# Three reorderings in a one-core, two-block transformer kernel: a projection tile ahead of a turned softmax, half a gate tile ahead of a suffix sum, and attention outputs split ahead of the next pair's logs

## The reference, cut to what matters

```
att = einsum(q * exp(b - b_mid), k * exp(b_mid - b));  att = where(causal, att, 0)
kv  = einsum(k * exp(b_last - b), v);  states by state = decay * state + kv
o   = att @ v + (q * exp(b)) @ states          # then a norm over each head and a gate
y   = softmax(q k / 8 + bias) v                # 8 heads
```

```
z = q k * 64 ** -0.5
log_beta = log_sigmoid(z);  log_rem = where(mask, log_sigmoid(-z), 0)
after = cumsum(log_rem, reverse) - log_rem
a = where(mask, exp(log_beta + after), 0);  o = a @ v
merged = sigmoid(gates[:1024] + b) * (o_diff @ w_o_diff) + sigmoid(gates[1024:] + b) * (o_sb @ w_o_sb)
```

## Time and profile before

| | |
|---|---|
| median of three runs | 1620.82 us |
| the profiled execution | 1622.88 us, its span 1621.1 us |
| PE busy, share of the span | 1449.0 us, 89% |
| DVE busy | 763.2 us, 47% |
| ACT busy | 578.3 us, 36% |
| mean granted TensorE clock | 0.949 |
| chain that ended last | PE 66%, DMA 18%, DVE 10%, ACT 4% |
| mixer, from the end of vm to the merge | 131.6 to 223.7 us |
| stick-breaking loop and what leads to it, layer 0 | 873 to 951 us |
| the same, layer 1 | 1286 to 1364 us |

### The profile page before, as it was taken

One profiled execution on the slowest core, in us unless ns is written; L12 is line 12 of the kernel. 1 busy time (PEld: TensorE's weight loads), 2 busy tenths in 40 slices (PEclk: granted clock), 3 DMA queues, 4 the chain that ended last, 5 costly groups with the idle time before them and its releaser, 6 DMA issues.

```text
span 1621.1 us, 23932 instructions
## 1 busy us (share of the span) xinstructions
PE 1449.0 (89%) x10631; PEld 1206.0 (74%) x10631; DVE 763.2 (47%) x1088; ACT 578.3 (36%) x708; POOL 2.9 (0%) x8
## 2 busy tenths in 40 slices
PE   7998999899767777677899899999999988999998
PEld 5696899755433434333888799999988878999997
DVE  2546564421101101101786676666367757765642
ACT  2452552221100100000546655434243665544431
POOL 0000000000000000000000000000000000000000
PEclk9997999999988988889999999999999999999999
DMA  6553147499999999999534335556534323546540
GB/s 206 208 187 120 53 156 314 185 406 426 427 427 426 427 427 427 425 427 416 180 131 150 111 107 177 185 169 221 192 121 141 119 105 117 195 156 204 188 155 27
DMA packets 116272, 374.56 MB, mean 231 GB/s; under 512 B 7767, under 2 KB 53127, under 8 KB 103623
## 3 DMA queue, kind: packets, MB, share of 16 engines
q1 hardware_dynamic: 112199, 370.70, 59.6%
q0 software_dynamic: 528, 2.04, 0.4%
q10 hardware_dynamic: 3440, 0.25, 0.2%
HBM read 371.92 MB, written 1.06 MB: 230 GB/s over the span
## 4 chain that ended last, share of the span: by engine, by line
PE 66%; DMA 18%; DVE 10%; ACT 4%; issue 1%; ACTq 1%; SPq 1%; DVEq 0%
PE bank L605 33%; DMA ring<-in_w_exp_up 10%; PE bank L1161 7%; PE bank L629 4%; DVE parts L1640 3%; PE bank L979 3%; DMA tail_hn<-in_w_exp_up 3%; DMA SZ<-in_w_exp_up 3%; PE bank L827 2%; DMA ring<-in_w_in 2%; PE bank L949 2%; PE bank L1006 2%; PE bank L583 2%; PE bank L651 2%; ACT parts L1255 1%
## 5 line engine op out<-in xcount | busy, mean ns | idle before, releaser
L605 PE MATMUL bank<-hnr,parts 128*128 128x256 f32 x4032 | 500.0, 286 | 7.6 <-DVE Gr L1792 6.8
L605 PEld LDWEIGHTS bank<-hnr,parts 128*128 128x128 f32 x4032 | 492.9, 194 | 13.4 <-DVE Gr L1792 7.2
L1640 DVE TENSOR_TENSOR parts<-ring,parts 128x2048 fp32r<-128x2048 f32 x148 | 333.7, 2288 | 129.4 <-ACT parts L1255 127.9
L1255 ACT ACTIVATE parts<-ring 128x2048 fp32r<-128x2048 f32 x146 | 271.5, 1902 | 105.5 <-PE bank L1161 58.7
L979 PE MATMUL bank<-ring,TMP 128*32 128x512 f32 x608 | 88.9, 734 | 47.9 <-DMA ring<-in_w_exp_up 47.2
L605 PE MATMUL bank<-SKr,parts 128*128 128x256 f32 x960 | 119.9, 288 | 8.6 <-DVE SKr L2031 5.8
L605 PEld LDWEIGHTS bank<-SKr,parts 128*128 128x128 f32 x960 | 118.6, 196 | 9.2 <-issue 9.1
L1161 PE MATMUL bank<-Gr,parts 128*128 128x256 f32 x640 | 115.3, 283 | 0.0
L1986 DVE COPY KV<-bank 128x256 f32<-128x256 f32 x16 | 6.8, 425 | 219.7 <-PE bank L966 219.7
L979 PEld LDWEIGHTS bank<-ring,TMP 128*32 128x32 f32 x608 | 23.5, 130 | 105.4 <-issue 90.2
L1161 PEld LDWEIGHTS bank<-Gr,parts 128*128 128x128 f32 x640 | 99.9, 192 | 0.0
(11 more groups left out here) (324 smaller groups left out, 1637.4 us busy)
## 6 DMA issues: line engine op xcount, KB each, us to landing
ring<-in_w_in SPq DMA_DIRECT2D x60, 1024.0 KB, 7.3
ring<-in_w_ffn_in SPq DMA_DIRECT2D x44, 1024.0 KB, 7.3
ring<-in_w_exp_gate SPq DMA_DIRECT2D x19, 2048.0 KB, 39.7
ring<-in_w_exp_up SPq DMA_DIRECT2D x19, 2048.0 KB, 44.2
ring<-in_w_exp_down SPq DMA_DIRECT2D x18, 2048.0 KB, 39.3
ring<-in_w_ffn_out SPq DMA_DIRECT2D x20, 1024.0 KB, 6.1
G<-in_w_exp_gate SPq DMA_DIRECT2D x7, 2048.0 KB, 38.6
tail_hn<-in_w_exp_up SPq DMA_DIRECT2D x7, 2048.0 KB, 43.1
```

Of the source, the lines that this page charges most:

```text
L605: m = mm(b(name)[:, T * half:T * half + T], part(chunk, ws)[:, k, P * mt:P * mt + P], src[xs][:, k, :], start=k == 0 and i == 0, stop=k == ...
L1255: A(parts[:, 2 * (r % 2), 2048 * i:2048 * i + 2048], ring[:, CHUNK[chunk][0], 2048 * i:2048 * i + 2048], ACT.Copy).then_inc(high_made, 1)
L1640: v.tensor_tensor(parts[:, 2 * (r % 2) + 1, at], ring[:, CHUNK[chunk][0], at], parts[:, 2 * (r % 2), at].bitcast(F32), ALU.subtract).then_ ...
```

## The change

There are five moves; no instruction is added or taken away but for waits. (1) The 48 matmuls of zg0 go ahead of mt_0. (2) In the mixer, DVE does the products with the decays ahead of low(zg0), vm0 and vm1, and low(zg1) after both norms; PE's waits for v1 and vm1 go to where they are used; ACT does high(zg1) after the first two softmaxes, and waits for io ahead of reading zg0, since z1 overlays the states. (3) Ahead of the loop in each layer, the first of ga1's two tiles goes ahead of ba0. (4) In the loop, second_highs goes ahead of sb_exps on ACT and second_lows ahead of sb_logs_of on DVE. (5) The second half of high(gb1) goes ahead of the gate bias of head 3.

```diff
-    g += [..., "ke", "ko", "mt_0", "oe", "oo", "ie", "io", "ms2"]
-    g += ["zg0", "gn0", "gn1", "mo0", "mt_1", "ms3", "zg1"]
+    g += [..., "ke", "ko", "zg0", "mt_0", "oe", "oo", "ie", "io", "ms2"]
+    g += ["gn0", "gn1", "mo0", "mt_1", "ms3", "zg1"]
...
 PE, mixer
-            emptied(pe, "v1")
-            emptied(pe, "vm1")
             causal_scores("ms0", qm, km, 0)
...
             emptied(pe, "kt")
+            emptied(pe, "v1")
             (ke, ko)
+            group_f("zg0", "zg0", 0)
             pe.wait_ge(prob_ready, 1)
             causal_turn("mt_0", prob[0])
             (oe, oo, ie, io)
             causal_scores("ms2", qm, km, 2)
-            group_f("zg0", "zg0", 0)
...
+            emptied(pe, "vm1")
             moba_out(0)
...
 PE, layers
                 diff_turn(3)
+                split_tile("ga0" + x, hn_parts, "ga1" + x, 2)
                 sb_after_sum(0)
-                group_f("ga0" + x, "ga1" + x, 1)
+                split_tile("ga0" + x, hn_parts, "ga1" + x, 3)
...
 ACT, mixer
             high("zg0")
-            high("zg1")
             take("kt", kdt.rearrange("p a b -> p (a b)"))
             causal_exp(0, [prob[0]])
             causal_exp(1, [prob[1]])
+            high("zg1")
             take_turned("mt_0", 0)
+            full(act, "io")
             take("zg0", two(z1, 0))
...
 ACT, loop over h
+                    if h in (2, 4, 6):
+                        second_highs(f"bo{h // 2 - 1}{x}", h // 2 - 1)
                     if h in (0, 2, 4):
                         sb_exps(h + 2)
                     if h < 7:
                         sb_weights(h + 1)
                     if h in (0, 2, 4):
                         sb_softplus(h + 2)
-                    if h in (2, 4, 6):
-                        second_highs(f"bo{h // 2 - 1}{x}", h // 2 - 1)
...
+                    if h == 3:
+                        high("gb1" + x, [1])
                     (gates)
-                    if h in (2, 3):
-                        high("gb1" + x, [h - 2])
+                    if h == 2:
+                        high("gb1" + x, [0])
...
 DVE, mixer
             take("km1", two(km, 1))
-            low("zg0")
-            take("vm0", vm[:, 0, :])
-            take("vm1", vm[:, 1, :])
             (products with the decays, memsets)
+            low("zg0")
+            take("vm0", vm[:, 0, :])
+            take("vm1", vm[:, 1, :])
...
-            low("zg1")
             moba_logits(0)
             (ae, ao)
             moba_logits(1)
+            moba_norm(0)
             (states)
-            moba_norm(0)
             moba_norm(1)
+            low("zg1")
...
 DVE, loop over h
                         sb_mask(h + 1)
+                    if h in (2, 4, 6):
+                        second_lows(f"bo{h // 2 - 1}{x}", l + 1, h // 2 - 1)
                     if h in (0, 2, 4):
                         sb_logs_of(h + 2)
                         sb_logs_of(h + 3)
...
-                    if h in (2, 4, 6):
-                        second_lows(f"bo{h // 2 - 1}{x}", l + 1, h // 2 - 1)
```

More of the change, by code:

```diff
@@ L117, in group_plan @@
     g += ["qk0", "qk1", "alr", "v0", "v1", "alpha", "r0", "r1", "qm0", "qm1", "km0", "km1", "vm0", "vm1"]
-    g += ["kt", "ms0", "ae", "ao", "ms1", "ke", "ko", "mt_0", "oe", "oo", "ie", "io", "ms2"]
-    g += ["zg0", "gn0", "gn1", "mo0", "mt_1", "ms3", "zg1"]
+    g += ["kt", "ms0", "ae", "ao", "ms1", "ke", "ko", "zg0", "mt_0", "oe", "oo", "ie", "io", "ms2"]
+    g += ["gn0", "gn1", "mo0", "mt_1", "ms3", "zg1"]
     for h in range(2, 8):
```

## The result

| | before | after |
|---|---|---|
| median (lowest to highest, runs) | 1621.07 us (1620.76 to 1622.02, 4) | 1591.74 us (1590.83 to 1592.65, 4) |
| the profiled execution, its span | 1622.88 us, 1621.1 us | 1591.38 us, 1589.6 us |
| PE busy | 1449.0 us | 1434.4 us |
| DVE, ACT busy | 763.2, 578.3 us | 762.5, 578.0 us |
| mean granted clock | 0.949 | 0.959 |

The ratio of the times is 0.982, with a 95% interval of 0.9805 to 0.9835. The kernel became 29.3 us faster; forecast were 1593.3 us and a gain of 27.5. PE does the same matmuls in 14.6 us less. Not all of that is gain: 3.8 us of it lie between the mixer's merge and layer 0, a stretch that is only 0.8 us shorter. In the stretches that the change reorders, up to the merges, PE is idle for 18.7 us less and busy for 14.3 us less; in the merges of the two layers it is busy for 4.1 us more. DVE and ACT do the same work.

What follows compares the result with a forecast made beforehand. TensorE holds two thirds of the chain of waits, DMA most of the rest; PE's waits and slow clock were the target. Mixer 9.5 + layers 18 = 27.5 us off 1622.88 gives 1595.4, as a median 1593.3; range 1583 to 1606.

Steps and rivals of the forecast that it cites:

- The walk: Layer 0's loop, followed step by step in its trace: merge starts at 940.5 instead of 951.15, 10.7 us gained.
- The walk of DVE's tail: Layer loop: DVE's work from Ln's end at 919.0 through the first first_lows, 21.4 us, making PE wait 2.6 at the merge.
- The table loads: Layers: three ACT table loads on the path; with the skill's drain two layers would lose 8.3 us, near 1601.6; left out.
- The clock at the merge: Each layer's merge: one slow stretch behind PE's wait, 1.7 us, cutting the layer's gain from 10.7 to 9.0 us.
- the two loops' term: Both layers' loops: 9.0 us gained in each, 18 together, bounds 18 to 21.4.
- The mixer: Waits ahead of kt and mt_0 go and zg1 starts earlier: 9.5 us taken, within 6.7 to 13.7.
- half of the loop's gain comes back as waits: Rival, layer loops: the second pair's waits stay, 5 us a layer, with 6.7 of the mixer 16.7, time 1604; 14%.
- the mixer gains nothing: Rival, mixer: the clock stays low from 135.8 through zg0 and the heads' sums; gain 2 + 18 = 20, time 1601; 13%.
- the clock stays low through the loop over heads: Rival, mixer: small matmuls and turned softmaxes keep 1.2 GHz, seven groups cost 41 us, time 1634; 3%.
- the sign of being wrong: Mixer: the forecast would be wrong if the clock in 145 to 165 us stood at 0.50.
- the end doesn't move: Rival, whole kernel: waits move but some queue taken for following sets the end, time within 0.2%; 4%.
- an Abs 7.2 us earlier: Layer loop: with high(gb1)'s half no longer behind gb0's bias, Abs of heads 6 and 7 starts at 914.85, not 922.05.

Runs made afterwards that it cites:

- a_roots: The kernel after with three half-width reciprocals of heads 0 and 1 moved from DVE's tail into its idle time in heads 2, 3 and 4; 1583.86 us.
- a_fill: The kernel after with 22 extra matmuls, whose results nobody reads, ahead of the merge in each layer; 1587.81 us.
- m_zg0: The kernel before with only zg0's 48 matmuls moved ahead of mt_0, with the bank order and ACT's wait for io that go with it; 1616.74 us.
- a_both: The kernel after with zg0's second tile behind ms2 and the three half-width reciprocals moved into DVE's idle time; 1578.47 us.
- m_order: The kernel before with the mixer's new order on DVE and ACT and PE's moved waits, but zg0 left behind ms2; 1613.40 us.
- l_logs: The kernel before with move (4) alone: second_highs ahead of sb_exps and second_lows ahead of sb_logs_of; 1605.50 us.
- m_only: The kernel before with the mixer's moves (1) and (2) alone; 1611.49 us.
- l_nogb1: The kernel after without move (5): the second half of high(gb1) is back behind gb0's gate bias; 1591.03 us.
- a_split: The kernel after with 24 of zg0's matmuls ahead of mt_0 and the other 24 behind ms2, covering DVE's squares; 1587.95 us.

## Why the prediction was right, point by point

**The loop.** The walk put the merge 10.7 us earlier, and it came 10.9 earlier in both layers. Its three waits were 0.8 to 1 us ahead of ba2 (measured 1.02), 1.1 ahead of ba6 (1.31) and 2.6 ahead of the merge (2.89), each on the instruction named. The walk of DVE's tail, 21.4 us, can be read off directly. The end of it in the chain of waits of the kernel after, layer 0 (start, duration, what):

```profile
904.64 0.53 ACT TMP L1493
...
905.20 0.57 DVE tail_hn L2137
...
909.51 1.68 DVE SQ L1783
...
913.18 1.67 DVE SQ L1783
...
915.36 1.67 DVE SQ L1783
...
919.36 1.67 DVE SQ L1783
...
921.54 4.40 DVE parts L1644 x2
925.94 0.61 DVE Gr L1790
926.69 3.33 PE bank L827 x14
```

From ACT's Ln at 904.64 the chain runs over DVE, but for two exponentials on ACT, to first_lows, whose end at 926.56 lies 21.4 us behind the Ln's end at 905.17. a_roots shows that it is this tail that sets the merge. Before, PE met the merge without a wait, so the tail was hidden.

**The table loads.** On the new path, too, the load starts at 903.35 and the activation behind it at 904.64, 1.29 us later. By the Trainium skill (ScalarE: Activation LUTs, What ACT_TABLE_LOAD costs), with a drain of about 1.38 us besides, the estimate was 1601.6 us. The trace doesn't agree on the drain: it shows none behind the load, nor ahead of it (the exponential before it ends at 903.33), and the time was 10 us lower.

**The clock at the merge.** Booked were 1.7 us for each layer; measured 2.7 and 1.45, 4.1 in all against 3.4. a_fill confirms the cause. In all the two loops' term, 18 us, came out at 17.6.

**The mixer.** This is the term that was mis-sized: 9.5 us taken, within 6.7 to 13.7, and 11.2 measured. Two parts were too careful. First, zg0 started 4.05 us behind vm's end and not about 5.4 (137 against 131.65), since the matmuls between kt and ko ran at full clock too: the 32 of L740 took 0.98 us, and 1.61 at half speed in m_zg0. Second, I took the slow end for the small matmuls because the clock had been low through them before. They ran the first 4 us at full speed. That oe to io took 6.3 us, near the 6.1 given for full speed, is luck: the named row (32 in 3.7 us) makes 6.5 for 56 of them, and here the last of them ran at half speed. With the clock up throughout they take 5.3 (139.24 to 144.52 in a_both). One part was too hopeful: the sums over heads ran at half speed (3.78 us, and 1.88 at full in m_order), so from their start to zg1 it took 6.87 us (148.67 to 155.54) and not 3.85. The wait for the squares, 1.39 us, was near the walked 1.

**The rivals.** That half of the loop's gain comes back as waits is ruled out by l_logs, which cleared the second pair of gaps too, in both layers. That the mixer gains nothing is ruled out by m_only's 9.3 us. That the clock stays low through the loop over heads didn't happen: it is back at 154.7, and zg1 takes 6.02 us. But the sign of being wrong that was set for it, 0.50 in 145 to 165 us, came true for about ten of the twenty us, and the forecast held all the same. That the end doesn't move is ruled out by the time. One slow stretch for each gap, as booked, was right in this sum, but the runs below show that it can't be relied on.

**Where a step was smaller than it read.** Move (5) stood in the walk as the cause of an Abs 7.2 us earlier. Nearly all of that came from move (4), which brought the whole of PE forward; by l_nogb1 the half of gb1 is worth 0.7 us in a layer, less than the clock at a merge moves by itself from one layer to the next (25.99 and 24.74 us for the same 192 matmuls).

## What to carry to other kernels

When a bank's release waits in an engine's list behind work that itself waits (here 0.42 us of subtraction behind a round trip to ACT's Ln), put the release ahead: one such move made 15 of 29 us. Then walk the engine that the bound engine will wait for next up to the merge: it says where the bound engine will wait instead, and which work to pull out of that tail (the reciprocals, 7.9 us more). A gap on PE can cost more than its length: look at the matmuls behind it at both clocks, and price the gap by filling it before reordering anything.

## What the runs showed of the hardware that was not expected

**The clock fell inside small matmuls though PE was not idle.** In the kernel after it fell at 144.5 us, inside 64-row matmuls, with PE busy without a gap since 22.45 us, and came back at 154.7; in m_only it was low from 142.3 to 152.5. In a_both the same instructions kept 1.00. What decides between the two is open. It needs no fetch: in a_split the clock fell at 142.7, and the DMA share was 0.00 from 142 to 144.

**Equal gaps did not cost the same.** Two stretches of l_logs, ahead of and behind ba0 and ba6:

```profile
874.00:880.00 6.00, 5.09 (x41) 5.07 (x42) 5.74 (x9) 5.02 (x7) 0.00 (x0) 1.00 0.01 1
920.00:928.00 8.00, 6.74 (x36) 6.23 (x37) 7.20 (x12) 3.40 (x4) 0.00 (x0) 0.79 0.36 145
```

The gap of 2.57 us ahead of ba0 left the clock at 1.00, where the same gap of 2.58 us in the kernel before had brought it down; the shorter one of 2.03 us ahead of ba6 was followed by half speed. In l_nogb1 a gap of 2.03 us ahead of ba6 lowered it in layer 1 and not in layer 0. What decides is open here too.

**Idle time filled with unread matmuls made both kernels faster**, by 3.9 and 9.2 us, with nothing else changed.

**A reciprocal is dear on DVE.** 128x256 takes 1.67 us in the chain above and 128x128 takes 0.94 us, where the two multiplications of 128x256 behind it (one instruction, L1784) take 0.48.
